# A diffusion backbone with attention and Hyena layers: skip weights in the Hyena filters, gates that read PSUM, reordered Hyena stages, a fourth PSUM bank and a rearranged prologue

## What is computed

```
def hyena_filters(n, w1, b1, w2, b2, w3, freq):
    ...
    h = jnp.sin(freq[0] * (feats @ w1 + b1))
    h = jnp.sin(freq[1] * (h @ w2 + b2))
    h = (h @ w3).astype(jnp.float32).reshape(n, 2 * HY_ORDER, D_MODEL)
    ...
    return h * jnp.exp(-t * deltas[None, :])[:, None, :]

def bidir_long_conv(z, h_fwd, h_bwd, skip):
    ...
    filt_full = jnp.concatenate([h_fwd, jnp.zeros_like(h_fwd[:1]), h_bwd[:0:-1]], axis=0)
    zf = jnp.fft.rfft(z.astype(jnp.float32), n=2 * n, axis=1)
    ff = jnp.fft.rfft(filt_full, n=2 * n, axis=0)
    y = jnp.fft.irfft(zf * ff[None], n=2 * n, axis=1)[:, :n]
    return (y + z.astype(jnp.float32) * skip.astype(jnp.float32)).astype(z.dtype)

    # in mixer_hyena
    u = dwconv_centred(h @ w_in, conv_w, conv_b)
    v, x1, x2 = jnp.split(u, HY_ORDER + 1, axis=-1)
    z = x1 * bidir_long_conv(v, filt[:, 0], filt[:, 1], skip[0])
    z = x2 * bidir_long_conv(z, filt[:, 2], filt[:, 3], skip[1])
    return z @ w_out
```

## Time and profile before

| | us |
|---|---|
| median of 3 runs | 1448.31 |
| fastest and slowest run | 1447.42, 1449.3 |
| the profiled execution, its own time | 1449.06 |
| its span, first to last instruction | 1447.3 |
| TensorE busy | 1377.5 (95%) |
| VectorE busy | 899.7 (62%) |
| ScalarE busy | 617.2 (43%) |
| GpSimd busy | 122.9 (8%) |
| mean granted clock of TensorE | 0.983 of full |

### The profile page before, as it was taken

How to read it: one execution, slowest core, us unless ns; L and a number is a source line. 1 busy time by engine, 2 the same in 40 slices (tenths; PEclk the granted TensorE clock), 3 DMA queues, 4 the chain that set the end, 5 groups by cost and what they waited for, 6 DMA issues and landing times. The chain is left out here.

```text
span 1447.3 us, 18140 instructions
## 1 busy us (share of the span) xinstructions
PE 1377.5 (95%) x6672; PEld 1133.5 (78%) x6672; DVE 899.7 (62%) x1291; ACT 617.2 (43%) x919; POOL 122.9 (8%) x149
## 2 busy tenths in 40 slices
PE   8989999999999999999998998898999999999996
PEld 2568788988878888888877787787887888888885
DVE  6878769977665555554466999988363333333333
ACT  3645446664362433415445434424445233252441
POOL 1761120002000000000100000000100000000011
PEclk9999999999999999999999999999999999999998
DMA  9535251119166565655212222230312323223221
GB/s 366 197 131 176 83 164 44 45 60 331 46 204 203 185 205 185 199 193 166 89 71 73 78 83 73 88 103 29 117 44 87 102 88 102 87 101 101 87 87 58
DMA packets 48265, 178.48 MB, mean 123 GB/s; under 512 B 5863, under 2 KB 6183, under 8 KB 45768
## 3 DMA queue, kind: packets, MB, share of 16 engines
q1 hardware_dynamic: 45192, 164.51, 33.4%
q0 software_dynamic: 3008, 13.11, 2.8%
HBM read 164.49 MB, written 10.49 MB: 121 GB/s over the span
## 5 line engine op out<-in xcount | busy, mean ns | idle before, releaser
L1727 PE MATMUL bank<-hhi,whi 128*128 128x512 f32 (+1 forms) x936 | 353.0, 377 | 9.3 <-ACT scratch L973 5.6
L1729 PE MATMUL bank<-hhi,wlo 128*128 128x512 f32 (+1 forms) x936 | 350.2, 374 | 0.0
L1728 PE MATMUL bank<-hlo,whi 128*128 128x512 f32 (+1 forms) x936 | 350.1, 374 | 0.0
L686 ACT ACTIVATE whi<-raw 128x1024 fp32r<-128x1024 f32 x180 | 189.5, 1054 | 216.2 <-PE bank L1729 199.4
L1109 DVE TENSOR_TENSOR wlo<-raw,whi 128x1024 fp32r<-128x1024 f32 x180 | 222.1, 1234 | 94.6 <-ACT whi L686 93.4
L1727 PE MATMUL bank<-ghi,whi 128*128 128x512 f32 x576 | 224.3, 389 | 4.7 <-DVE glo L1652 2.8
L1729 PE MATMUL bank<-ghi,wlo 128*128 128x512 f32 x576 | 224.1, 389 | 0.0
L1728 PE MATMUL bank<-glo,whi 128*128 128x512 f32 x576 | 224.1, 389 | 0.0
L1727 PEld LDWEIGHTS bank<-hhi,whi 128*128 128x128 f32 x936 | 177.0, 189 | 41.3 <-ACT whi L686 10.0
L1729 PEld LDWEIGHTS bank<-hhi,wlo 128*128 128x128 f32 x936 | 177.0, 189 | 31.4
L1728 PEld LDWEIGHTS bank<-hlo,whi 128*128 128x128 f32 x936 | 177.1, 189 | 30.8
(11 more groups left out here) (272 smaller groups left out, 2009.9 us busy)
## 6 DMA issues: line engine op xcount, KB each, us to landing
raw<-in_wpack SPq DMA_DIRECT2D x180, 512.0 KB, 3.5
araw<-in_apack SPq DMA_DIRECT2D x40, 512.0 KB, 3.6
amore<-in_apack SPq DMA_DIRECT2D x36, 512.0 KB, 3.5
ablk<-in_ahead SPq DMA_DIRECT2D x8, 1024.0 KB, 11.0
spectra<-scratch SPq DMA_DIRECT2D x16, 512.0 KB, 3.2
araw<-spectra POOLq DMA_DIRECT2D x8, 1024.0 KB, 5.0
fs<-in_fw SPq DMA_DIRECT2D x2, 1024.0 KB, 11.2
x<-in_xT SPq DMA_DIRECT2D x1, 2048.0 KB, 11.9
```

The costliest lines, as they stand in the source:

```text
L686: A(whi[:, s, :], raw[:, r, :], ACT.Copy).then_inc(hi_done, 1)
L1727: mm(o, lh, rh, start=first, stop=False)
L1728: mm(o, lh, rl, start=False, stop=False)
L1729: return mm(o, ll, rh, start=False, stop=last)
```

## The change

- The skip weights are loaded as rows (4 KB, and two of 2 KB by GpSimd) and added to row 0 of the filter's even part; the skip products and their column constants go, and so does `conv`.
- `gate` multiplies the inverse in PSUM by the taps directly. An inverse waits for the gate that frees its bank.
- TensorE's order in a stage is transposes, one unit, forward, two inverses, forward, two inverses, three units. The last three units come before the last four inverses. The other engines' orders follow; the products of a spectrum are parted by a unit's taps and gate.
- The Hyena output's operand goes into `hhi` and `hlo`, in the order of the chunks.
- The fourth unit behind a boundary writes bank 2.
- At a boundary, the first root is moved and the sums of the second half are parted.
- In the prologue, the orders of VectorE, ScalarE and TensorE change, the reciprocal is cut into four, tiles go between halves of transforms, and two matmuls on zeros are issued first.
- At attention's start, the reciprocal and the eight small products move forward, the two copies move one step back.

```diff
-        FIRST_BANKS = (AB[:, 0, :], AB[:, 1, :], SC[:, 0, :])
+        FIRST_BANKS = (AB[:, 0, :], AB[:, 1, :], SC[:, 0, :], B2[:, :])
...
+            sp.dma_start(tap2[0:1, :, :], skips[:, 0:2, :]).then_inc(skip_in[0], 16)
             load_head(0)
...
             for n in range(8):
                 filter_los(n)
+                if n == 0:
+                    load_skip(2)
...
             pool.wait_ge(xadd_done, 3)
+            load_skip(3)
...
                 if i >= 2:
                     act.wait_ge(tlo_done, 1)
+                    act.wait_ge(row0_done, 2)
...
+            filter_odd(0, 0)
             weight_his(2)
-            filter_odd(0, 0)
+            filter_odd(0, 1)
             weight_his(3)
-            filter_odd(0, 1)
...
                 if n == 1:
                     values_hi(1)
+                if n == 2:
                     act.wait_ge(csum_done, 1)
...
                     for i in range(4):
+                        if h and i == 2:
+                            x_root(b, 0)
...
-                    if h == 0:
-                        x_root(b, 0)
...
                 act.wait_ge(dft_done, m + 1)
                 if m:
-                    act.wait_ge(spec_lo, 4 * m)
+                    act.wait_ge(spec_full, 4 * m)
                 A(S[:, 9, :], SC[:, 1, :], ACT.Copy).then_inc(odd_done, 1)
+                if m:
+                    act.wait_ge(spec_lo, 4 * m - 3)
...
+            z_hi(0)
             for k in range(4):
-                z_hi(k)
                 n = 4 * (k + 1)
+                if k:
+                    spectrum_hi(2 * k - 1)
...
-                for i in range(n + 2, n + 6):
+                for i in range(n + 2, n + 5):
                     hy_unit(i)
-                spectrum_hi(2 * k + 1)
+                    if i == 18:
+                        hy_prep(20)
+                if k < 3:
+                    z_hi(k + 1)
+                hy_unit(n + 5)
+            spectrum_hi(7)
...
+            act.wait_ge(unit_done, U_HY + HY_UNITS)
+            act.wait_ge(tap_done, 20)
+            for j in range(4):
+                z3_his(j)
+            hy_unit(22)
+            z3_his(4)
+            hy_prep(21)
+            hy_unit(23)
+            z3_his(5)
+            for j in (6, 7):
+                act.wait_ge(tap_done, 17 + j)
+                z3_his(j)
+            hy_prep(22)
             hy_prep(23)
...
+            nc.vector.memset(S[:, 8, :], 0.0).then_inc(warm_set, 1)
...
-                    nc.vector.tensor_scalar_mul(e0, e0, 0.5).then_inc(row0_done, 1)
+                    if n != 4:
+                        dve.wait_ge(skip_in[max(n // 4 - 1, 0)], 16)
+                    STT(e0, e0, 0.5, SKIP[n // 4], ALU.mult, ALU.add).then_inc(row0_done, 1)
...
+            def x_inverse(i):
+
+                dve.wait_ge(sd_done, 1)
+                part = S[:, 9, i * P:(i + 1) * P]
+                nc.vector.reciprocal(part, part).then_inc(rs_done, 1)
...
             weight_sums(2)
+            filter_out(0, 0)
             weight_sums(3)
-            filter_out(0, 0)
+            filter_out(0, 1)
             weight_los(2)
             modulation(0)
-            filter_out(0, 1)
             weight_los(3)
-            prep(0, 0, 0)
             filter_outs(1)
-            prep(1, 1, 1)
             filter_tile(8)
             filter_tile(9)
             filter_outs(2)
+            prep(0, 0, 0)
             filter_tile(10)
+            x_inverse(0)
+            filter_out(3, 0)
             filter_tile(11)
+            x_inverse(1)
+            filter_out(3, 1)
...
-                dve.wait_ge(conv_done, n - 7)
-                TT(y[:, n % KC, :], y[:, n % KC, :], UNIT_TAPS[n % 2], ALU.mult).then_inc(tap_done, 1)
+                dve.wait_ge(inv_done, n - KC + 1)
+                v, t = (w.rearrange("p (m two) -> p two m", two=2) for w in (y[:, n % KC, :], UNIT_TAPS[n % 2]))
+                STT(v, (B2, B3)[n % 2][:, :].rearrange("p (two m) -> p two m", two=2), 1.0 / 512, t, ALU.mult,
+                    ALU.mult).then_inc(tap_done, 1)
...
             for k in range(1, 4):
                 n = 4 * (k + 1)
+                spectrum_added(2 * k - 1)
                 z_los(k)
+                spectrum_ends(2 * k - 1)
                 hy_prep(n - 1)
                 taps(n)
+                spectrum_sums(2 * k)
+                gate(n)
                 taps(n + 1)
-                conv(k - 1, 0)
-                gate(n)
+                gate(n + 1)
                 hy_prep(n)
-                spectrum_sums(2 * k)
-                conv(k - 1, 1)
-                gate(n + 1)
                 spectrum_products(2 * k)
-                conv(k - 1, 2)
-                conv(k - 1, 3)
+                hy_prep(n + 1)
+                spectrum_added(2 * k)
                 spectrum_ends(2 * k)
-                hy_prep(n + 1)
                 spectrum_sums(2 * k + 1)
                 hy_prep(n + 2)
                 if k == 3:
                     hy_prep(19)
-                spectrum_products(2 * k + 1)
                 hy_unit(n + 2)
-                hy_unit(n + 3)
-                spectrum_ends(2 * k + 1)
+                if k == 3:
+                    hy_prep(20)
+                spectrum_products(2 * k + 1, n + 3)
+            spectrum_added(7)
+            spectrum_ends(7)
...
+            pe.wait_ge(warm_set, 1)
+            for i in range(2):
+                mm(B3[:, :], S[:, 8, 0:P], S[:, 8, :], start=True, stop=True)
...
+            filter_tile(8)
+            filter_tile(9)
+            filter_dft(2)
+            pe.wait_ge(gen_used, 19)
+            pe.wait_ge(xadd_done, 4)
+            mm(B2[:, :], ones, XSQ[0][:, 0, :], start=True, stop=True).then_inc(xss_done, 1)
+            filter_tile(10)
+            filter_dft(3)
...
                 x_sums(b, 0)
+                x_sums(b, 1, range(4))
                 x_rows(b, 0)
-                x_sums(b, 1)
+                x_sums(b, 1, range(4, KC))
...
+            def fourth_unit(u0):
+
+                unit(u0 + 3, 3, FIRST_BANKS[3], hhi, hlo, evacs=u0).then_inc(unit_done, 1)
...
                 if 4 * k + i >= 2:
-                    pe.wait_ge(conv_done, 4 * k + i - 1)
+                    pe.wait_ge(tap_done, KC + 4 * k + i - 1)
...
             for k in range(1, 4):
                 transposes(k)
+                hy_unit(4 * k + 5)
+                forward(k, 0)
                 inverse(k - 1, 0)
-                forward(k, 0)
                 inverse(k - 1, 1)
+                forward(k, 1)
                 inverse(k - 1, 2)
-                forward(k, 1)
                 inverse(k - 1, 3)
-                for n in range(4 * k + 6, 4 * k + 10):
+                for n in range(4 * k + 6, 4 * k + 9):
                     hy_unit(n)
+            hy_unit(21)
             hy_unit(22)
+            hy_unit(23)
             for i in range(4):
                 inverse(3, i)
-            hy_unit(23)
```

More of the change, by code:

```diff
@@ L301, in build @@
         inv_done = sem("inv_done")
[L302 to L303 removed]
+        skip_in = [sem(f"skip_in{n}") for n in range(3)]
         z3_hi = sem("z3_hi")
@@ L1605, in spectrum_products @@
                 own.wait(k)
+                if between is not None:
+                    hy_unit(between)
                 e3 = es[:, 3, :]
@@ L2098, in _ @@
             forward(0, 1)
-            for n in range(6, 10):
+            for n in range(6, 9):
                 hy_unit(n)
```

177 lines of the change are left out of this document (85 added, 92 removed).

## The result

The changed kernel takes 1409.78 us, the median of 4 runs (1409.05 to 1411.3), against 1447.87 for the kernel before (4 runs, 1446.8 to 1449.3): a ratio of 0.9739, 95% interval 0.9727 to 0.9751. The profiled execution took 1409.05 us with a span of 1407.0. The forecast was 1414; against its own profiled execution it had 34.6 us to win, and 40.0 came.

What follows compares the result with a forecast made beforehand. TensorE, busy 1377.5 of 1447.3 us, bounds the kernel: 70 us of waiting and some half clock can be won. Terms of 34.6 off 1449.06 give 1414.5, or 1413.7 against the median; predicted 1414, range 1401 to 1431.

Steps and rivals of the forecast that it cites:

- Hyena's three stages: A unit and a forward transform between transposes and first inverse cover TensorE's wait for VectorE's low parts; 13.0 us won.
- Hyena's tail: After the last spectrum, three units ahead of the last inverses and operand chunks in order cut TensorE's waits; 6.0 us won.
- fourth bank: A fourth unit covers the first evacuation at both MLPs: 5.7 us, 3.0 of clock at the second; Hyena's start loses 1.7.
- boundaries: At three boundaries, moving the first root and parting the second half's sums wins 0.5 us each, 1.5 in all.
- attention's entry: Eight small products, a reciprocal and two copies leave the path to attention's first maximum and second exponential; 1.6 us won.
- opening: Two matmuls on zeros before the first adaLN block bring TensorE's clock up to 3.4 us sooner; 1.5 us won.
- prologue: From 57.2 to 118 us, reordered outputs, a cut reciprocal and tiles filling transforms win 4.0 us despite a 3 us wait.
- A: The forecast itself, 1414 us, own range 1406 to 1422: each wait that goes has a named cover; chance 0.58.
- B: All fits, hardly a half-clock stretch is left, no loss at Hyena's start; 1403 us, chance 0.14.
- C: VectorE stays the bound in Hyena's stages, its low parts late for the first inverse again; 1427 us, chance 0.21.
- D: The fourth bank fails because the fourth unit waits for its own weights; 1422 us, chance 0.04.
- E: Slower than before: fewer but longer TensorE pauses bring half clock behind every stage's transposes and gates; 1452 us, chance 0.03.

Runs made afterwards that it cites:

- Experiments 2: Changed kernel with a useless 0.69 us product put on VectorE ahead of each of 12 gates, four a stage; 1414.37 us.
- 9: Changed kernel with TensorE's whole order of the three Hyena stages put back as before, fused gates and tail kept; 1427.42 us.
- experiments 3: Changed kernel with the fourth bank taken back at Hyena's first units alone, both MLPs keeping it; 1408.86 us.
- 4: Changed kernel with the taps of Hyena's unit 3 ahead of preparation 3 on ScalarE and VectorE; 1406.59 us.
- 11: Changed kernel with ten matmuls on idle operands ahead of the last group of Hyena's first transposes; 1406.24 us.
- experiment 5: Changed kernel with the fourth bank taken back at both MLPs, Hyena keeping it; 1417.86 us.
- Experiment 8: Changed kernel without the two matmuls on zeros at the opening; 1410.73 us.

## Why the prediction was right

By its own steps. "Traces" is the shift table, "undone" the matching experiment's median against 1409.78, and the last column the same stretch in that experiment's trace against the changed kernel's.

| term | predicted (bounds) | traces | undone | its trace |
|---|---|---|---|---|
| Hyena's three stages | 13.0 (8.4 to 15.4) | 14.3 | 17.6 | 16.4, 4.4 of it new |
| Hyena's tail | 6.0 (3 to 6.6) | 6.4 | not tried | |
| fourth bank, MLPs' waits | 5.7 | 6.0 | 8.1, with the next | 7.7, with the next |
| clock at the second MLP | 3.0 (0 to 3.5) | 2.9 | | |
| clock at Hyena's first units | -1.7 (-1.7 to 0) | -1.2 | -0.9 | -1.2 |
| boundaries | 1.5 (-1 to 5) | 5.7 | 5.3 | 3.9, 2.6 of it the edit's |
| attention's entry | 1.6 (0 to 3) | 2.5 | 3.9 | 3.0 |
| opening | 1.5 (-0.3 to 2) | 0.1 | 0.95 | 0.0 |
| prologue | 4.0 (0 to 8) | 4.5 | 5.9 | 5.7 |

The traces' column adds up to 41.2 us at the last boundary, and 0.8 is given back in it.

**The stages.** Right in the mechanism and nearly in size. The first of the three won 3.8 (51.3 to 47.5), the second 5.2; the third can't be cut from the tail by a matmul, and is given the 5.3 that its wait of 3.7 and its clock were worth, which leaves 6.4 for the tail. "It fits by 0.8 us" is what the trace shows. VectorE's last low part and the inverse that needs it, changed kernel, second stage:

```profile
867.17 0.68 DVE L1662 TENSOR_TENSOR glo<-scratch,ghi 128x512 fp32r<-128x512 f32 x1
...
868.65 0.28 PE L1758 MATMUL bank<-t2hi,ghi 128*128 128x256 f32 x1
```

It ends at 867.85, 0.80 ahead of 868.65. The once-only loss of 0.8 came too, as 0.60 + 0.19 in the first of the three. The 0.8 taken off every stage for small slips (2.4 in all) did not; instead the first stage lost some 0.8 more than its waits. So the term came out 1.3 short. Experiments 2 and 9 say which half of the edit did it: mostly the order, worth some 12; VectorE's lighter load is worth 2.2 under the old order and 4.6 under the new one. The gate takes 0.69 us, as sized from the convolution.

**The fourth bank.** Right at both MLPs and at Hyena, where the sum had to take a loss: a pause of 2.82 us behind one of 1.14, 4.0 in two parts where one of 4.5 was forecast, and 1.2 us of clock. (The 4.2 us for the fifth unit's weights adds up to 4.1, which changes nothing.) The Trainium skill (TensorE: Matmul & The Clock Gate, "Why this matters for your kernels") warns of long idle gaps between bursts of matmuls; this trace and experiments 3, 4 and 11, which end the gap or split it and are at full clock, agree. Only the price was sized too high, 1.7 for 1.2.

**The boundaries.** The failed step is "Taken 0.5 each". The waits moved as said, from the root to the squares, and gave next to nothing (8.5 us to 8.2). What the step left out is the clock: 0.84, 0.91 and 0.91, worth 3.4, 1.8 and 1.7 us, were there in the trace of before and not read. Of the 5.4 us by which the sum fell short, 4.2 are here. But not all of it is the change's doing. Behind the sums, where the edit is, the three won 2.0, 2.0 and 0.2, the first two with half clock behind the pause of 1.9; another 1.4 is half clock that began ahead of any wait, which the edit doesn't touch. That part is luck of the two executions.

**Attention's entry.** The same: 0.7 of wait was won, and the rest is the clock behind it, which I had left in.

**The opening.** The failed step is that "the rise should come up to 3.4 sooner". With the two matmuls the first block is over at 15.37, without them at 15.38. The pace was better than in the trace of before in both, by 0.87 us at the first filter tile, and that lead ended at VectorE's filter, which the prediction didn't name.

**The prologue.** Right by luck of the mean more than by its steps: the sum of x squared waits 1.75, not 3, but GpSimd's low parts (L597) hold a transform for 1.98, which wasn't foreseen. One of two half-clock stretches went.

**The rivals.** A holds. B (hardly any half clock, 1403) came true in part: the tail is 0.2 short of its value and the boundaries are above theirs, the stages lie half way to them, and Hyena's start and the prologue kept it away. C fell: TensorE, not VectorE, bounds the second stage; in the first VectorE is busy 46.7 of 47.5 us, and TensorE waits 0.8. D and E fell: no wait at the fourth unit, and two half-clock stretches inside the kernel by the clock column instead of eleven, not more.

The undone parts add up to 47.3 us with the tail at 6.4, more than the 38.1 that the whole won. Read from the matching stretches of their traces they add up to 41.9, near the 41.2 between the two kernels. So most of what is too much is clock that an undone kernel's execution lost at places which the edit doesn't touch, at boundary 1 and Hyena's start above all. A better version came out of it: experiment 4, at 1406.6 us, moves two lines. With the filler of experiment 11 it was not tried.

## What to carry over

Before pricing waits, list the stretches at half clock, and look whether a pause stands ahead of each: here 12 us of 40 were clock, and both terms that came out well above their forecast were such stretches beside a wait that itself changed little. When an experiment undoes a part, read the stretch that it touches, and not only the total. Price a moved block by the spare time at the next thing that needs its result, to a tenth of a microsecond: 0.8 forecast, 0.80 found. Instructions fewer on the lighter engine win little until the order lets them, and an early gain is worth only what the next late thing lets through.

## What the runs showed of the hardware

The same pause is followed by half clock in one execution and not in another. At the MLPs pauses of 2.8 us each lost clock at the second alone in the kernel before, and at the first alone in experiment 5. Experiment 8 shows it at places whose instructions are the same as in the changed kernel, the boundaries at 720 and at 1020 us:

```profile
720.00:740.00 20.00, 17.29 (x81) 14.04 (x81) 13.18 (x24) 7.20 (x14) 0.00 (x0) 0.91 0.19 77
1023.00:1041.00 18.00, 16.32 (x78) 13.06 (x77) 11.47 (x17) 7.03 (x14) 0.00 (x0) 0.91 0.07 25
```

The changed kernel's are at 1.00. And no pause stood ahead of these two. The first of them from its small matmuls on, in experiment 8 and then in the changed kernel:

```profile
721.84 1.95 PE L1983 MATMUL bank<-consts,scratch 128*128 128x1 f32 x16
723.65 1.63 PE L1998 MATMUL bank<-t2hi 128*128 128x512 f32 x3
...
730.38 1.97 PE L2023 MATMUL bank<-scratch,consts 128*128 128x256 f32 x8 [1.03 <-ACT scratch L951]
```

```profile
722.01 1.95 PE L1987 MATMUL bank<-consts,scratch 128*128 128x1 f32 x16
723.82 0.94 PE L2002 MATMUL bank<-t2hi 128*128 128x512 f32 x3
```

The granted clock falls to half of full speed (1.2 of 2.4 GHz) at about 723.6 and is back by 727.1, ahead of the boundary's first wait. What TensorE did before it fell was two matmuls of 4 columns and sixteen of 1, from 721.52 to 723.65. The changed kernel did the same 0.2 us later and kept full clock. So a single trace says what a stretch cost, but not that the place will have it each time; I had read them as fixed. The runs of one kernel spread by 1 to 5 us, which one or two stretches explain in size; that they are the cause was not shown.
